# A two-layer decoder trunk on one core: more identity products in the last expert pairs, and another order of three steps in the second layer's softmax

## The reference, cut to what matters

```python
def reference(x, ...):
    for i in range(DEPTH):                                   # DEPTH = 2
        mix = moba_attention(...) if i % 2 == 0 else nsa_attention(...)
        x = layer_norm(DEEPNORM_ALPHA * x + mix, ln_g[i, 0], ln_b[i, 0])
        ffn = grouped_moe(x, router_w, router_b, moe_w_gate[i], moe_w_up[i], moe_w_down[i])
        x = layer_norm(DEEPNORM_ALPHA * x + ffn, ln_g[i, 1], ln_b[i, 1])
    return x

def grouped_moe(x, ...):
    ...
    def expert_block(args):
        xt, e = args
        hid = jax.nn.silu(xt @ w_gate[e]) * (xt @ w_up[e])
        return hid @ w_down[e]                               # 1024 x 512, 1024 x 512, 512 x 1024
    ...

def nsa_attention(x, ...):
    ...
    q, kc, vc, ks, vs, kw, vw, g = jnp.split(proj, ...)
    ...
            p_s = jax.nn.softmax(s_s, axis=-1)...            # selected blocks, keys ks, values vs
            p_w = masked_softmax(s_w + bias_w, valid_w)      # window, keys kw, values vw
            return gc[..., 0:1] * o_c + gc[..., 1:2] * o_s + gc[..., 2:3] * o_w
```

## Time and profile before

| | |
|---|---|
| median of three runs | 1193.33 us (1193.14 to 1196.06) |
| the profiled execution | 1195.33 us |
| its span in the trace | 1193.5 us |
| PE / DVE / ACT / POOL busy | 85% / 30% / 15% / 5% |
| moved by DMA | 449.12 MB, mean 376 GB/s |
| mean granted TensorE clock | 0.926 |

### The profile page before, as it was taken

The page is one execution under the profiler, slowest core; times in us unless marked ns, Lnnn a source line. Parts: engine busy times, 40 slices in busy tenths (PEclk is TensorE's granted clock), DMA queues, the critical chain, the costliest instruction groups (busy, mean ns, idle before and its releaser), DMA issues.

```text
span 1193.5 us, 18920 instructions
## 1 busy us (share of the span) xinstructions
PE 1014.6 (85%) x7872; PEld 565.5 (47%) x7872; DVE 356.2 (30%) x888; ACT 184.5 (15%) x474; POOL 55.7 (5%) x133
## 2 busy tenths in 40 slices
PE   9999999976698966678899999999866898766765
PEld 7595544543343533344599655444533434423432
DVE  4745612221111111111567775213111111111112
ACT  1023211100010100000321663111100000000001
POOL 1012010000000000000100230100000000000000
PEclk9999999987799987789999999999977899878898
DMA  9937899999999999999992719999999999999994
GB/s 352 373 142 288 343 394 419 426 427 429 427 427 427 428 427 428 428 424 423 371 362 84 283 35 364 391 418 427 427 427 426 428 427 427 427 427 427 427 423 191
DMA packets 59351, 449.12 MB, mean 376 GB/s; under 512 B 4579, under 2 KB 10980, under 8 KB 32636
## 3 DMA queue, kind: packets, MB, share of 16 engines
q1 hardware_dynamic: 57248, 442.52, 90.2%
q0 software_dynamic: 1680, 4.88, 1.2%
q10 hardware_dynamic: 332, 0.42, 0.1%
HBM read 446.72 MB, written 1.07 MB: 375 GB/s over the span
## 4 chain that ended last, share of the span: by engine, by line
PE 55%; DMA 40%; DVE 2%; ACT 1%; issue 1%; SPq 1%; DVEq 0%
PE bank L1220 15%; DMA ring<-in_moe_w_up 14%; DMA ring<-in_moe_w_down 11%; DMA ring<-in_moe_w_gate 10%; PE bank L1001 7%; PE bank L1184 5%; PE bank L1072 5%; DMA bias<-in_moe_w_up 5%; PE bank L1305 3%; PE bank L1281 2%; PE bank L1469 2%; PE bank L1320 2%; PE bank L1041 1%; PE bank L1292 1%; PE bank L1496 1%; PE bank L1063 1%
## 5 line engine op out<-in xcount | busy, mean ns | idle before, releaser
L1220 PE MATMUL bank<-ring,work 128*32 128x256 f32 (+1 forms) x2656 | 336.4, 493 | 106.9 <-DMA ring<-in_moe_w_gate 35.5
L1220 PEld LDWEIGHTS bank<-ring,work 128*32 128x32 f32 (+1 forms) x2656 | 154.5, 136 | 244.4 <-issue 217.2
L1950 DVE TENSOR_TENSOR work<-work,bank 128x256 f32<-128x256 f32 (+1 forms) x32 | 15.6, 488 | 520.6 <-PE bank L1220 520.6
L1305 PE MATMUL bank<-ring,work 128*32 128x512 f32 x576 | 91.9, 627 | 11.6 <-DMA ring<-in_moe_w_down 7.2
L1220 PE MATMUL bank<-softmax_area,work 128*32 128x256 f32 (+1 forms) x352 | 65.8, 503 | 33.8 <-DMA ring<-in_moe_w_gate 25.4
L1963 DVE TENSOR_TENSOR xs<-xs,bank 128x512 f32<-128x512 f32 x112 | 71.1, 684 | 41.8 <-PE bank L1323 23.6
L1220 PE MATMUL bank<-bias,work 128*32 128x256 f32 (+1 forms) x384 | 78.1, 499 | 0.0
L1184 PE MATMUL bank<-work,acc 128*128 128x128 f32 (+1 forms) x448 | 75.5, 323 | 0.0
L1184 PEld LDWEIGHTS bank<-work,acc 128*128 128x128 f32 x448 | 66.0, 191 | 16.6 <-issue 11.5
L1220 PEld LDWEIGHTS bank<-softmax_area,work 128*32 128x32 f32 (+1 forms) x352 | 31.9, 141 | 66.6 <-issue 60.9
L2388 ACT COPY work<-bank 128x256 f32<-128x256 f32 (+1 forms) x32 | 13.6, 425 | 319.4 <-PE bank L1257 252.3
(11 more groups left out here) (331 smaller groups left out, 1273.9 us busy)
## 6 DMA issues: line engine op xcount, KB each, us to landing
ring<-in_moe_w_gate SPq DMA_DIRECT2D x44, 2048.0 KB, 29.2
ring<-in_moe_w_up SPq DMA_DIRECT2D x40, 2048.0 KB, 28.6
ring<-in_moe_w_down SPq DMA_DIRECT2D x36, 2048.0 KB, 29.2
softmax_area<-in_moe_w_down SPq DMA_DIRECT2D x8, 2048.0 KB, 25.1
ring<-in_moe_w_down SPq DMA_DIRECT2D x12, 1024.0 KB, 8.4
ring<-in_moe_w_gate SPq DMA_DIRECT2D x12, 1024.0 KB, 9.3
bias<-in_moe_w_gate SPq DMA_DIRECT2D x6, 2048.0 KB, 34.6
softmax_area<-in_moe_w_up SPq DMA_DIRECT2D x6, 2048.0 KB, 27.7
```

What stands on the lines that cost most here:

```text
L1220: last = mm(bank[2 + k][row:row + cap, 0:width], xgT_of(group_of[i])[:, t, at + e * cap:at + (e + 1) * cap], w[e](t)[:, part * width:(part ...
L1305: last = mm(bank[5][row:row + CAP_NARROW, :], hidT_narrow[:, m, CAP_NARROW * e:CAP_NARROW * (e + 1)], w[e](m)[:, n * 512:(n + 1) * 512], s ...
```

## The change

Three edits. In `gate_up`, the last pair of each layer gets three identity products of 512 columns into bank 2 ahead of its gate block, behind the wait for ScalarE's silu of pair 14 (which frees bank 2), and four instead of one into bank 3 ahead of its up block. In the table, the products `("values", REST)` go from step 3 to step 4. On ScalarE, the copy of bank 5 goes ahead of the exponentials in every unfilled step from 2 on, and stays behind them in the others. With the table changed, the unfilled steps of the second layer are 2, 3, 5, 6, 9, 11, 13, 15 and 17.

```diff
-  {0: [("proj", ("keys", REST))], 1: [...], 3: [("proj", ("values", REST))], 7: [("out", 0)], ...
+  {0: [("proj", ("keys", REST))], 1: [...], 4: [("proj", ("values", REST))], 7: [("out", 0)], ...
...
                 if "gate" in blocks:
                     pe.wait_ge(silu_ready, PAIRS * l + i)
+                    if i == PAIRS - 1:
+                        keep_warm(3, b=2)
                     block(0, range(KT)).then_inc(gate_done, 1)
...
                 if i == PAIRS - 1:
                     acc_to_psum(l)
-                    keep_warm(1, b=3)
+                    keep_warm(4, b=3)
                 block(1, range(KT)).then_inc(up_done, 1)
...
             def softmax_steps(l):
+                def copy_probsT(j):
+                    act.wait_ge(probsT_ready[l], j + 1)
+                    after(act, pv_done[l], j - 1)
+                    s_.copy(probsT[:, 2 * (j % 2) + 1, :], bank[5][:, 0:3 * P]).then_inc(probsT_act, 1)
...
                 for s in range(n_steps + 2):
...
+                    unfilled = not beside[l].get(s)
+                    if s >= 2 and unfilled:
+                        copy_probsT(s - 2)
                     if s < n_steps:
                         ... the exponentials ...
...
-                    if s >= 2:
-                        j = s - 2
-                        act.wait_ge(probsT_ready[l], j + 1)
-                        after(act, pv_done[l], j - 1)
-                        s_.copy(probsT[:, 2 * (j % 2) + 1, :], bank[5][:, 0:3 * P]).then_inc(probsT_act, 1)
+                    if s >= 2 and not unfilled:
+                        copy_probsT(s - 2)
```

More of the change, by code:

```diff
@@ L658, in build @@
                    5: [("out", 0)], 6: [("out", 1)], 7: [("out", 2)], 8: [("out", 3)], 9: [("out", 4)], 10: [("out", 5)]},
-                  {0: [("proj", ("keys", REST))], 1: [("proj", ("values", LAST_SELECTED)), ("cmp", 0)], 3: [("proj", ("values", REST))], 7: [("out", 0)], 8: [("out", 1)], 10: [("out", 2)], 12: [("out", 3)],
+                  {0: [("proj", ("keys", REST))], 1: [("proj", ("values", LAST_SELECTED)), ("cmp", 0)], 4: [("proj", ("values", REST))], 7: [("out", 0)], 8: [("out", 1)], 10: [("out", 2)], 12: [("out", 3)],
                    14: [("out", 4)], 16: [("out", 5)], 18: [("out", 6)]}]
```

## The result

The changed kernel is slower: 1198.68 us in the median of eight runs (1196.24 to 1201.52) against 1193.36 for the kernel before, a ratio of 1.0047 with a 95% interval of 1.0038 to 1.0056. I had forecast 1191.9 and no measurable change. The profiled execution took 1201.52, 6.19 more than that of before; it is the slowest of the eight, 2.8 above their median.

A forecast was written before the change was run, and what follows sets the result against it. Expert weight loads were taken to bound most of the span, the core's work mattering at layer ends and in attention. Terms -1.03, 0 and -0.35 summed to -1.4: 1193.33 to 1191.9 us, own range 1190.9 to 1192.9, with rivals 1190.0 to 1194.4.

The forecast's parts named there:

- The wait covers 1.9: Second layer's last gate: of 2.70 us of new products, the wait for gate weights hides 1.9; gate starts 0.79 late.
- Cost 0, hidden by a landing wait of 1.67: First layer's last pair: up block starts 1.19 us late, but the wait for the last down quarter hides it.
- Second layer, products: Last pair: up block at full clock ends 1.41 us earlier; the last down quarter's landing leaves 1.03 of that.
- First layer, products: Last pair: gate at full clock, 3.66 instead of 5.28 us; the layer's end unmoved, 0.
- Softmax: Second layer's steps 3 to 6: a 1.19 us wait goes, waits of 0.6 and 0.25 come; sum -0.35.
- (b): Clock does not follow the products: first layer's gate and second layer's up block stay slow; +1.1, 1194.4 us; chance 0.12.
- (c): Last pair's slow up block is not in every execution; only -0.35 is left, 1193.0 us; chance 0.15.
- (a): Both pieces give all: softmax waits hidden, last down quarter lands sooner; -2.6, 1190.7 us; chance 0.15.
- (d): Softmax copies still come late and the moved products cost: +1.25 - 1.03 = +0.2, 1193.5 us; chance 0.08.

The follow-up runs named there:

- e5: Changed kernel plus 22 never-run identity products in the first layer's overflow branch, moving the code block's end behind pair 14's up block: 1193.03 us, ratio 0.9992.
- e6: Kernel before plus 28 and 10 never-run identity products in the overflow branches, moving the code block's end behind pair 14's up block: 1192.18 us, ratio 0.9991.
- e9: Changed kernel plus four identity products right behind the branch, ahead of pair 14's up block, and 56 never-run ones in each overflow branch: 1194.47 us, ratio 1.0008.
- e10: Kernel before plus only four identity products right behind the branch, ahead of pair 14's up block: 1192.75 us, ratio 0.9993.
- e4: Changed kernel without the extra products, so only the table's step and ScalarE's order differ from the kernel before: 1193.64 us, ratio 1.0005.
- e1: Kernel before plus 6 and 12 never-run identity products in the overflow branches, shifting code as in the changed kernel: 1193.99 us, ratio 1.0005.
- e8: Kernel before plus only the three products ahead of the last gate block, and 25 never-run ones in the first layer's overflow branch: 1192.49 us, ratio 0.9989.
- e12: Changed kernel without the three added products ahead of the up block, plus 25 never-run ones in the first layer's overflow branch: 1192.33 us, ratio 0.9989.
- e2: Changed kernel plus 58 and 53 never-run identity products in the overflow branches, putting its code back where it stood before: 1194.12 us, ratio 1.0005.
- e7: Kernel before plus only three extra products ahead of the last up block, and 25 never-run ones in the first layer's overflow branch: 1194.67 us, ratio 1.0007.

## Why the prediction was wrong, step by step

**The step that failed** is where the extra products were costed by their cover: "The wait covers 1.9" in the second layer, and "Cost 0, hidden by a landing wait of 1.67" in the first. Both take TensorE to reach the last pair as early as before. I counted what the added instructions execute, and not that they lengthen the program, here in the copy that never runs as well. So I had no term for the wait for code, though its 0.80 and 0.96 stood in the trace of before, and the section of the Trainium skill named above speaks of a stall behind a taken branch, if only for the target's own block.

**Second layer, products: forecast -1.03, came out +3.1.** From the first record of pair 14's up block to the end of the last down quarter took 41.99 us before (1139.92 to 1181.91) and 45.06 now (1143.05 to 1188.11). Pair 14's up block ends 4.84 later against its own start (11.27 us instead of 6.43): 2.63 of it are the longer wait for code, the rest records at a lower clock (0.50 and 0.55 granted, 0.64 and 1.00 before); whether the longer wait lowered it is not shown. The products add 5.1 (2.58, and 3.43 instead of 0.9). Against that go the landing waits of 1.92 and 3.11, which vanish, and 1.75 on the up block, which took 3.63 instead of 5.38 as forecast. 4.84 + 5.1 - 5.03 - 1.75 = 3.2, where 45.06 - 41.99 is 3.07; the rest lies in the short pieces between. And the gain itself can't be counted on: with the code out of the way on both sides (e5 and e6) it is not there.

**First layer, products: forecast 0, came out +2.5.** The same stretch took 41.48 (535.35 to 576.83) and now 44.01 (536.17 to 580.18). The gate did run at full clock, in 3.59 instead of 5.28, as forecast; but the wait that was to hide the rest, the last one in this row of before, is gone:

```profile
575.73 1.06 PE L1305 MATMUL bank<-ring,work 128*32 128x512 f32 x8 [1.67 <-DMA ring<-in_moe_w_down]
```

Pair 14's up block took 10.21 instead of 6.79, 2.20 of it the longer wait for code. With 5.1 for the products, 1.69 back on the gate, and the waits of 2.59 and 1.67 gone, 3.42 + 5.1 - 1.69 - 4.26 = 2.6.

**Softmax: forecast -0.35, came out -0.02.** The mechanism was right: the 1.19 is gone, and waits in steps 3 and 6 came in its place. They were mis-sized, 0.77 and 0.36 instead of 0.6 and 0.25. The profile puts the end of both down to VectorE's copy, which ended at 669.54 and 681.42; GpSimd's scaling, on which I had rested the second, ended 0.04 earlier each time, so which of the two held TensorE is not settled.

**The rest.** Pair 14's up block of the first layer began 0.82 later already, ahead of the changed products (in the profiles of the other kernels but e9 and e10 it begins between 535.10 and 536.94), and the stretch between the two layers' places gave 0.2 back. 0.82 + 2.5 - 0.02 - 0.2 + 3.1 = 6.2, the difference of the two profiled executions; the medians differ by 5.3.

**The rivals.** (b) came nearest in its time (1194.4) with the wrong mechanism: the clock followed. (c) was right in what it said, that the slow up block is not in every execution: of the seven profiled kernels with a single product ahead of the second layer's last up block, it took 5.35 in two (before and e4, behind 3.11 and 2.46 us of idle time) and 3.66 in five (e1, e6, e8, e10 and e12, behind 0.10 to 1.72). That is the likely reason why even e5 gains nothing over e6. (a) and (d) did not happen. What none of them held is a cause upstream of the last pair.

**What stays open:** what holds the second code load back until 5.6 to 6.4 us after that of the branch's target. It need not be the branch: in the eleven cases in which, by the count, the block ended within the first 16 records of the up block, the load after it began another 6.0 to 6.8 us later. And all 28 lie beside a weight stream of 418 to 431 GB/s; no run took that away.

## What to carry to other kernels

Added instructions also move the code behind them, and where a branch is taken, even instructions that never run can decide where an engine waits for code: look in the trace for waits on no signal behind a branch, and pad there before judging an edit. A cost of nothing rests on the engine's arriving early; ask what could make it late upstream, since two changes that cost nothing measurable one at a time (e1 and e2, ratios of 1.0005 each) can cost 0.47% together. And a gain read off a single profile, like a block at half clock, should be seen in a second execution before it is counted on.

## What the runs showed of the hardware

Behind the taken branch of these kernels come two code loads, not one. The target's block lets TensorE go on 2.65 to 2.68 us after its load starts (four cases); the next load starts 5.6 to 6.4 us after the target's (28 cases), and TensorE goes on 2.38 to 2.64 us after that start. If the target's block runs out before, TensorE stands, for up to 3.99 us here (e1). The Trainium skill's section named above calls the crossing of a block mostly hidden; behind this branch the measurement says otherwise.

TensorE's clock did not follow the length of an idle stretch alone. In e7 a gate block behind 3.22 us of waiting ran in 3.66 with 1.00 granted (first layer), while one behind 3.06 took 5.00 with 0.72 (second layer); in the kernel before, one behind 2.59 took 5.28 with 0.68.
